# Moving a matrix-vector product from GpSimd to VectorE, one multiply-add at fixed places between weight conversions

## The chip, the cores and the metric

The kernel runs on one core of a Trainium2 chip. The metric is the device time of one execution in microseconds. The engines are TensorE (PE in the profile, its weight loads PEld), VectorE (DVE), ScalarE (ACT), GpSimd (POOL) and the sync engine (SP), which issues every DMA. Each runs its own instruction stream in order, and they meet only at semaphores.

## The reference

The input is one sequence of 256 tokens of width 1024, in float32. The first block has four layers of three sublayers each: FFN, mixer (MLA attention, differential attention, a Mamba-2 SSM, MLA again), FFN. Every sublayer is modulated by a vector that depends only on the conditioning input c:

```
cond = jax.nn.silu(c)                                  # (1, 1024)
mod = (cond @ w_mod[i] + b_mod[i]).reshape(-1, 3, 3, 1024)
shift, scale, gate = mod_j[:, 0, None, :], mod_j[:, 1, None, :], mod_j[:, 2, None, :]
y = fn(x * (1 + scale) + shift)
x = layernorm(DEEPNORM_ALPHA * x + weight * gate * y, g, b)
```

The matrix w_mod has 1024 x 9216 elements per layer, so each sublayer needs a matrix-vector product of 1024 x 3072. A second block follows (a hybrid of dilated attention and retention, cross-attention over a memory, an FFN) that has no modulation.

## The kernel before

Tokens lie along the free dimension and features on the 128 partitions. All weights are streamed. `Plan` cuts each matrix into blocks of 128 x 2048 float32 (1 MB): a column block is 256 columns of all eight row chunks, a block of an output projection is two row chunks of all 1024 columns. Every product is done in three float32r matmuls (high by high, high by low, low by high), so each block passes through this line:

- SP loads it into `raw[b % 4]` (`load`, line 524), once the block four before it has been converted by VectorE (`w_lo`).
- ScalarE rounds it into `whi[b % 2]` in two halves (`convert`, line 644), once TensorE is done with block b - 2.
- VectorE subtracts, `wlo = raw - whi`, in two halves (`convert`, line 971; the instruction is line 979).
- TensorE does 48 matmuls a block (line 1502 in `three`).

In a stage, turn i of VectorE and ScalarE converts block i + 2 of it. The FFN is a stage "in" of 22 column blocks and a stage "out" of 11 row blocks, written as loops of four blocks by `walk`, with what lies ahead and behind peeled. Mixers are unrolled: diff has 12 column blocks ahead of its attention and 4 row blocks behind it, the SSM 8 (z), 12 (xbc, where VectorE also does a convolution) and 1, the scan, and 8 row blocks, and MLA 3, a norm of the latents, 4 (q, each of six small DMAs), 2 (kv), the attention and 4 row blocks. `splits(g)` is VectorE's loop of conversions in a mixer, `projected` the one of an output projection, `attend` its part of an attention.

Between two sublayers stands a layer norm (`dve_ln`, `pe_ln`). VectorE computes the sum, the mean, the variance, then the modulated input (`hf`, `H_lo`), and last `residual()`, which signals `ax_ready`.

While sublayer s runs, the modulation product of s + 1 is accumulated in `mod_acc`, 128 x 2 x 1536, two halves. Row chunk k (128 rows) and half h are an item, numbered 2k + h, 16 in all. Each item is a DMA of 768 KB into `mod_w[:, h, :]` (`load_mod`, line 537). Load u waits until item u - 2, the last that used this half of the buffer, has been added: semaphore `mod_used`. GpSimd waits for the load, then does one small tick, one product by the element of `cond` of this row chunk (line 624, in place), and one add into `mod_acc` (line 627). It works whenever data is there. In `pe_ln`, TensorE sums over the partitions with 24 matmuls of one column (line 1570, `mod_sums`), which signal `mod_sum`; after that GpSimd begins on the next sublayer.

The order of SP's queue is written out. In an FFN, `load_mod` of the items 0 to 9 follows the weight loads at every second block of "in", items 10 and 11 stand ahead of the first "out" load, and the other four come among the "out" loads. In a mixer, each weight load ahead of the output projection is followed by one modulation load, and all that are left follow the second load of the output projection.

Of the kernel before, what the change touches and what calls it, by code (L numbers as in the profile page):

```python
# [26 lines left out]
ALU = mybir.AluOpType  # L27
AX = mybir.AxisListType.X
ds = bass.ds

P = 128
# [4 lines left out]
DEPTH = 4  # L36
# [279 lines left out]
def program(nc, plan, A, out, first, second):  # L316
# [4 lines left out]
    with ctx:  # L321
        def sem(name):
            return ctx.enter_context(nc.semaphore(name))
# [45 lines left out]
        pool_tick = at("pool_tick", [P, 16], room(64))  # L369
# [89 lines left out]
        mod_used = sem("mod_used")  # L459
        dve_step, act_step, pool_step = sem("dve_step"), sem("act_step"), sem("pool_step")  # L460
# [34 lines left out]
        def _(sp):  # L495
# [50 lines left out]
            for st in steps:  # L546
# [41 lines left out]
                if st.kind in ("mla", "diff", "ssm", "hyb", "xatt"):  # L588
                    nxt = st.args[0] + 1 if st.kind not in ("hyb", "xatt") else 10 ** 6
                    todo = [(nxt, k, half) for k in range(DC) for half in range(2)] if nxt < plan.mods else []  # L590
                    for g in st.lin.values():
                        for b in range(g.b, g.b + g.n):
                            load(b)

                            late = g is st.lin["out"] and b == g.b + 1
                            while todo and (late or b < st.lin["out"].b):
                                load_mod(*todo.pop(0))
                                if not late:
                                    break
# [6 lines left out]
        @block.gpsimd  # L606
        def _(pool):

            n = min(plan.mods, SUB * DEPTH)
            if n > 1:  # L610
                pool.wait_ge(s["cond_ready"], 1)
                with pool.Fori(1, n) as sub:
                    pool.wait_ge(s["mod_sum"], sub * 2)
                    for k in range(DC):
                        for half in range(2):
                            pool.wait_ge(mod_loaded[half], sub * 128 + 16 * (k + 1) - 128)

                            nc.gpsimd.tensor_tensor(pool_tick[:, 2 * k + half:2 * k + half + 1], cond[:, 0:1], cond[:, 0:1], ALU.add)  # L618
                            w = mod_w[:, half, :]
                            if k == 0:  # L620
                                nc.gpsimd.tensor_scalar(mod_acc[:, half, :], w, cond[:, 0:1], 1.0, ALU.mult, ALU.mult)\
                                    .then_inc(mod_used, 1)
                                continue
                            nc.gpsimd.tensor_scalar(w, w, cond[:, k:k + 1], 1.0, ALU.mult, ALU.mult).then_inc(pool_step, 1)  # L624
                            pool.wait_ge(pool_step, sub * 14 - 14 + 2 * (k - 1) + half + 1)
                            pool.wait_ge(mod_used, sub * 16 + 2 * k + half - 1)
                            nc.gpsimd.tensor_tensor(mod_acc[:, half, :], mod_acc[:, half, :], w, ALU.add)\  # L627
                                .then_inc(mod_used, 1)
# [331 lines left out]
        def _(dve):  # L960
# [19 lines left out]

            def coefficients(sub, n):
# [157 lines left out]
            def dve_ffn(st, n):  # L1139
# [17 lines left out]
                def turn(i, it=None):  # L1157
                    convert(g.b + i + 2, it)
                    if i % 2 == 1:
                        product(i // 2, it)  # L1160
                    if i % 2 == 0 and i >= 2:
                        product_lo(i // 2 - 1, it)

                walk(dve, g, turn)
                product_lo(FP - 1)
                projected(st)

            def projected(st):
                g = st.lin["out"]
                walk(dve, g, lambda i, it: None if it is None and i >= g.n - 2 else convert(g.b + i + 2, it), 1, 2)  # L1170


            def attend(n, heads, scale, kind):
# [62 lines left out]
                for i in range(heads + 4):  # L1236
                    if i < heads:
                        maxima(i)
                    if 1 <= i <= heads:
                        normal(i - 1)  # L1240
                    if i >= 4:
                        output(i - 4)

            def dve_mla(st, n):
                splits(st.lin["latent"])
# [16 lines left out]
                splits(st.lin["q"])  # L1262
                splits(st.lin["kv"])
# [10 lines left out]
                attend(n, MLA_H, 192.0 ** -0.5, "mla")  # L1274
                projected(st)

            def splits(g):
                for i in range(g.n):
                    convert(g.b + i + 2)

# [5 lines left out]
            def dve_diff(st, n):  # L1286
                splits(st.lin["qk"])
                splits(st.lin["v"])
                attend(n, 8, 64.0 ** -0.5, "diff")
# [11 lines left out]
            def dve_ssm(st, n):  # L1301
                splits(st.lin["z"])
# [79 lines left out]
                projected(st)  # L1382
# [581 lines left out]
```

## Time and profile before

| | |
|---|---|
| median of 3 runs | 3269.76 us (3255.11 to 3269.94) |
| span of the profiled execution | 3259.7 us |
| the profiled execution's own time | not on the page; the runs' median is 10.1 us over its span |
| TensorE busy | 2803.8 us (86%) |
| VectorE busy | 2262.1 us (69%) |
| ScalarE busy | 1272.2 us (39%) |
| GpSimd busy | 1080.1 us (33%) |
| DMA | 576.21 MB, mean 177 GB/s |

A row of the view by groups reads: line, engine, operation, output<-inputs, shapes, count, then busy us and mean ns of one, then the idle time ahead of them and what ended it. A row of the view by windows reads: start:end, length, then busy us (and instructions) of PE, PEld, DVE, ACT and POOL, then the granted TensorE clock (1.0 is full speed), the DMA engines' share and GB/s; a "sum" row adds several windows, their length first. A row of a timeline reads: start, us, engine, line, operation, and in brackets the idle time ahead of it and who ended it. In the view by waits it is: who waited for whom, us in total, times, longest.

### The profile page before, as it was taken

The numbers are of one execution on the slowest core, as the hardware profiler recorded it, in microseconds if no ns is written. First come the engines' busy times: TensorE is split into PE (matmuls) and PEld (weight loads), VectorE is DVE, ScalarE is ACT, GpSimd is POOL, SyncE is SP. The second block draws the span as 40 slices with busy tenths as digits, with TensorE's granted clock in tenths as the row PEclk, the third lists the DMA queues.
The fourth block names the chain that finished last, engine by engine and source line by source line (L and its number), as shares of the span: only waits on it lengthen the run. The fifth ranks groups of instructions, "written<-read, shape, count | busy, mean of one in ns | idle before, by whom it ended". The sixth has DMA issues, their size and how long they took to land.

```text
span 3259.7 us, 52310 instructions
## 1 busy us (share of the span) xinstructions
PE 2803.8 (86%) x20687; PEld 2661.0 (82%) x20687; DVE 2262.1 (69%) x2608; ACT 1272.2 (39%) x1667; POOL 1080.1 (33%) x510
## 2 busy tenths in 40 slices
PE   3996689989885998997889899999579988869797
PEld 3996489989884998997864899899559988569797
DVE  6677667777788777787766677775866555674554
ACT  2433344344334443443332443443234434344443
POOL 0564605627382263473800056263550000000000
PEclk7997789989897899997985899899678998779898
DMA  8774437657562575664720376475343544124352
GB/s 293 248 256 139 153 111 249 235 191 261 186 220 71 191 258 181 240 254 149 264 92 0 120 254 246 168 260 198 124 144 130 180 177 155 52 78 143 129 180 91
DMA packets 355092, 576.21 MB, mean 177 GB/s; under 512 B 20175, under 2 KB 295818, under 8 KB 354826
## 3 DMA queue, kind: packets, MB, share of 16 engines
q1 hardware_dynamic: 354954, 574.29, 50.6%
q8 instruction: 97, 1.59, 0.2%
q14 instruction: 41, 0.34, 0.0%
HBM read 573.20 MB, written 1.05 MB: 176 GB/s over the span
## 4 chain that ended last, share of the span: by engine, by line
PE 69%; DVE 21%; issue 6%; ACT 3%; SPq 1%; DMA 0%; DVEq 0%; ACTq 0%
PE ps L1502 62%; DVE wlo L979 4%; ACT whi L642 2%; PE ps L1815 1%; PE ps L1640 1%; DVE hf L1123 1%; DVE H_lo L1128 1%; DVE acc L1094 1%; PE ps L1806 1%; DVE acc L1010 1%; DVE z L1133 1%; DVE z L1110 1%; DVE ax L1022 1%; DVE conv L1317 1%; PE ps L1667 1%
## 5 line engine op out<-in xcount | busy, mean ns | idle before, releaser
L979 DVE TENSOR_TENSOR wlo<-raw,whi 128x1024 fp32r<-128x1024 f32 x804 | 1292.5, 1624 | 708.8 <-ACT whi L642 705.1
L1502 PE MATMUL ps<-H_hi,whi 128*128 128x256 f32 x4256 | 1236.4, 291 | 164.3 <-DVE H_lo L1128 75.7
L642 ACT ACTIVATE whi<-raw 128x1024 fp32r<-128x1024 f32 x804 | 846.1, 1058 | 1333.6 <-PE ps L1502 1327.2
L1502 PE MATMUL ps<-H_lo,whi 128*128 128x256 f32 x4256 | 1228.3, 289 | 0.0
L1502 PE MATMUL ps<-H_hi,wlo 128*128 128x256 f32 x4256 | 1227.4, 288 | 0.0
L1502 PEld LDWEIGHTS ps<-H_hi,whi 128*128 128x128 f32 x4256 | 842.1, 198 | 176.4 <-issue 137.8
L1502 PEld LDWEIGHTS ps<-H_lo,whi 128*128 128x128 f32 x4256 | 842.6, 198 | 0.0
L1502 PEld LDWEIGHTS ps<-H_hi,wlo 128*128 128x128 f32 x4256 | 841.3, 198 | 0.0
L627 POOL TENSOR_TENSOR mod_acc<-mod_acc,mod_w 128x1536 f32<-128x1536 f32 x154 | 619.1, 4020 | 25.2 <-POOL mod_w L624 25.2
L1502 PE MATMUL ps<-A_hi,whi 128*128 (+1 forms) x1880 | 538.4, 286 | 51.2 <-DVE A_lo L1256 28.1
L618 POOL TENSOR_TENSOR pool_tick<-cond 128x1 f32<-128x1 f32 x176 | 113.9, 647 | 1309.6 <-PE ps L1570 766.5
L1502 PE MATMUL ps<-A_hi,wlo 128*128 (+1 forms) x1880 | 535.6, 285 | 0.0
L1502 PE MATMUL ps<-A_lo,whi 128*128 (+1 forms) x1816 | 517.8, 285 | 0.0
L1502 PEld LDWEIGHTS ps<-A_hi,whi 128*128 128x128 f32 x1880 | 365.1, 194 | 55.5 <-DVE A_lo L1256 28.9
L1502 PEld LDWEIGHTS ps<-A_hi,wlo 128*128 128x128 f32 x1880 | 364.9, 194 | 0.0
L1502 PEld LDWEIGHTS ps<-A_lo,whi 128*128 128x128 f32 x1816 | 352.9, 194 | 0.1
L624 POOL TENSOR_SCALAR mod_w<-mod_w,cond 128x1536 f32<-128x1536 f32 x154 | 319.3, 2073 | 0.0
L1570 PEld LDWEIGHTS ps<-K,mod_acc 128*128 128x128 f32 x576 | 111.0, 290 | 23.0 <-DVE mod_acc L1048 20.2
L1570 PE MATMUL ps<-K,mod_acc 128*128 128x1 f32 x576 | 106.4, 315 | 19.9 <-DVE mod_acc L1048 19.9
L1640 PE MATMUL ps<-KN,QN 128*128 128x128 f32 (+3 forms) x192 | 55.1, 472 | 42.8 <-DVE QRp L1273 28.3
L1101 DVE SCALAR_TENSOR_TENSOR z<-ps,gw,ax 128x256 f32<-128x256 f32 x96 | 44.9, 478 | 65.4 <-PE ps L1502 65.4
L681 ACT ACTIVATE prob<-prob,stat 128x128 f32<-128x128 f32 x80 | 34.8, 445 | 135.0 <-DVE stat L1197 135.0
(278 smaller groups left out, 2304.7 us busy)
## 6 DMA issues: line engine op xcount, KB each, us to landing
raw<-in_ffn_w_in_dram SPq DMA_DIRECT2D x176, 1024.0 KB, 5.1
mod_w<-in_w_mod_dram SPq DMA_DIRECT2D x180, 768.0 KB, 6.2
raw<-in_ffn_w_out_dram SPq DMA_DIRECT2D x88, 1024.0 KB, 6.0
raw<-in_w_gate_up_dram SPq DMA_DIRECT2D x22, 1024.0 KB, 5.0
raw<-in_ssm_w_in_dram SPq DMA_DIRECT2D x20, 1024.0 KB, 7.0
raw<-in_w_in_dram SPq DMA_DIRECT2D x14, 1024.0 KB, 4.9
raw<-in_diff_w_in_dram SPq DMA_DIRECT2D x12, 1024.0 KB, 5.9
raw<-in_w_down_dram SPq DMA_DIRECT2D x11, 1024.0 KB, 4.9
```

Source lines behind the costliest of these rows:

```text
L618: nc.gpsimd.tensor_tensor(pool_tick[:, 2 * k + half:2 * k + half + 1], cond[:, 0:1], cond[:, 0:1], ALU.add)
L624: nc.gpsimd.tensor_scalar(w, w, cond[:, k:k + 1], 1.0, ALU.mult, ALU.mult).then_inc(pool_step, 1)
L627: nc.gpsimd.tensor_tensor(mod_acc[:, half, :], mod_acc[:, half, :], w, ALU.add)\
L642: return nc.scalar.activation(dst, src, ACT.Copy)
L681: i = nc.scalar.activation(prob[:, h % 4, m * width + a:m * width + b], src, ACT.Exp, bias=stat[:, h % 4, 4 + 2 * m + t:5 + 2 * m + t], sc ...
L979: tt(wlo[b % 2][:, r], raw[b % RAW][:, r], whi[b % 2][:, r].bitcast(F32), ALU.subtract).then_inc(w_lo, 1)
L1010: link(tt(f, f if q > 1 else sq[:, 0:2, :], sq[:, 2 * q:2 * q + 2, :], ALU.add))
L1022: i = ts(ax[:, c, :], z[:, c, :], G2[:, c:c + 1], B2[:, c:c + 1], ALU.mult, ALU.add)
L1101: stt(z[:, c, :], ybank(g, c), gw[:, c:c + 1], ax[:, c, :], ALU.mult, ALU.add).then_inc(s["z_ready"], 1)
L1502: m = pe.matmul(out, l, r, start=first and i == 0, stop=last and i == 2, skip_group_check=rest)
L1570: m = pe.matmul(ps[:, b, o:o + 1], mod_acc[:, c // 12, c % 12 * P:c % 12 * P + P], ones[:, 0:1], start=True, stop=True)
L1640: m = pe.matmul(ps[:, b, o:o + keys], q[:, t * P:t * P + P], k[:, 0:keys], start=i == 0, stop=i == len(terms) - 1)
```

## The change

GpSimd's loop is replaced by one clearing of the accumulator for each sublayer, which waits for `mod_sum` and for the residual's `ax_ready` and signals `mod_clear`. VectorE does each item in one instruction, `mod_acc = mod_w * cond + mod_acc` (`modulate`), at a fixed place: in the FFN's "in" stage ahead of the conversion in every even turn from 2, items 10 and 11 in turn 0 of "out", items 12 to 15 in later turns of "out"; in MLA and diff one item behind each conversion of `splits` and one in each turn of `attend` until none is left; in the SSM eight items in z and eight behind the turns of the output projection. The FFN's and the other mixers' order of loads stays as it is; in the SSM the modulation loads now stand behind the loads of z and of the output projection.

```diff
-                            late = g is st.lin["out"] and b == g.b + 1
-                            while todo and (late or b < st.lin["out"].b):
+                            late = st.kind != "ssm" and g is st.lin["out"] and b == g.b + 1
+                            early = g is st.lin["z"] or g is st.lin["out"] if st.kind == "ssm" else b < st.lin["out"].b
+                            while todo and (late or early):
                                 load_mod(*todo.pop(0))
                                 if not late:
                                     break
...
-                with pool.Fori(1, n) as sub:
+                for sub in range(1, n):
                     pool.wait_ge(s["mod_sum"], sub * 2)
-                    for k in range(DC):
-                        for half in range(2):
-                            pool.wait_ge(mod_loaded[half], sub * 128 + 16 * (k + 1) - 128)
...
+                    pool.wait_ge(s["ax_ready"], sub)
+                    nc.gpsimd.memset(mod_acc[:, :, :], 0.0).then_inc(mod_clear, 1)
...
+            def modulate(sub, k, half, it=None):
+
+                u = 16 * sub + 2 * k + half
+                loaded = 128 * (sub - 1) + 16 * (k + 1)
+                dve.wait_ge(mod_loaded[half], loaded if it is None else loaded + 16 * it)
+                if k == 0:
+                    dve.wait_ge(mod_clear, sub)
+                dve.wait_ge(mod_used, u - 1 if it is None else u - 1 + 2 * it)
+                c = cond[:, k:k + 1] if it is None else cond[:, ds(it + k, 1)]
+                stt(mod_acc[:, half, :], mod_w[:, half, :], c, mod_acc[:, half, :], ALU.mult, ALU.add).then_inc(mod_used, 1)
...
                 def turn(i, it=None):
+                    if mods and i >= 2 and i % 2 == 0:
+                        modulate(mods, (i - 1) // 4, (i - 1) // 2 % 2, it)
                     convert(g.b + i + 2, it)
...
+                def turn_out(i, it):
+                    if mods and i == 0:
+                        modulate(mods, 5, 0)
+                        modulate(mods, 5, 1)
+                    if mods and i in (1, 3):
+                        modulate(mods, 6, i // 2, it)
+                    if it is not None or i < g.n - 2:
+                        convert(g.b + i + 2, it)
...
-            def splits(g):
+            def splits(g, mods=()):
                 for i in range(g.n):
                     convert(g.b + i + 2)
+                    if mods:
+                        modulate(*mods.pop(0))
```

`attend` and the SSM's `projected` get the same last two lines at the end of each turn.

## Rows read from the trace of the kernel before

**Rows 1.** The page: busy shares, and the chain by engine.

```profile
PE 2803.8 (86%) x20687; PEld 2661.0 (82%) x20687; DVE 2262.1 (69%) x2608; ACT 1272.2 (39%) x1667; POOL 1080.1 (33%) x510
PE 69%; DVE 21%; issue 6%; ACT 3%; SPq 1%; DMA 0%; DVEq 0%; ACTq 0%
```

**Rows 2.** By windows: norm, "in" and "out" of FFN 11, GpSimd idle.

```profile
2467.20:2483.30 16.10, 10.91 (x51) 10.33 (x52) 14.44 (x31) 8.09 (x13) 0.00 (x0) 0.58 0.20 66
2483.30:2611.60 128.30, 128.30 (x1057) 128.30 (x1058) 75.71 (x87) 59.23 (x69) 0.00 (x0) 0.99 0.53 177
2611.60:2675.50 63.90, 63.77 (x530) 63.36 (x528) 28.29 (x31) 22.86 (x22) 0.00 (x0) 1.00 0.60 217
```

**Rows 3.** By windows: sum of the "in" stages of the other seven FFNs.

```profile
sum 913.10, PE 906.26 PEld 903.28 DVE 714.45 ACT 413.06 POOL 496.10; mean PE 129.47 PEld 129.04 DVE 102.06 ACT 59.01 POOL 70.87
```

**Rows 4.** By windows: sum of the seven "out" stages.

```profile
sum 464.00, PE 449.14 PEld 447.72 DVE 291.70 ACT 160.14 POOL 200.77; mean PE 64.16 PEld 63.96 DVE 41.67 ACT 22.88 POOL 28.68
```

**Rows 5.** By windows: sum of six norms ahead of an FFN.

```profile
sum 102.50, PE 59.90 PEld 56.97 DVE 93.97 ACT 45.77 POOL 10.27; mean PE 9.98 PEld 9.49 DVE 15.66 ACT 7.63 POOL 1.71
```

**Rows 6.** By windows: sum of the four norms ahead of a mixer.

```profile
sum 72.20, PE 41.13 PEld 39.16 DVE 67.30 ACT 32.70 POOL 15.17; mean PE 10.28 PEld 9.79 DVE 16.83 ACT 8.18 POOL 3.79
```

**Rows 7.** Timeline of GpSimd in the first FFN.

```profile
160.57 3.52 POOL L627 TENSOR_TENSOR mod_acc<-mod_acc,mod_w 128x1536 f32<-128x1536 f32 x1 [0.16 <-POOL mod_w L624]
```

**Rows 8.** Timeline of VectorE at the same place.

```profile
160.72 4.45 DVE L979 TENSOR_TENSOR wlo<-raw,whi 128x1024 fp32r<-128x1024 f32 x1 [1.65 <-ACT whi L642]
```

**Rows 9.** VectorE's instructions on the tile wlo: min/median/max ns, first and last start.

```profile
L979 DVE TENSOR_TENSOR wlo<-raw,whi x804: 1204/1226/4539, 44.9 to 3228.1; 128x1024 fp32r<-128x1024 f32 x161
```

**Rows 10.** By windows: MLA's start to scores, diff's, SSM's z, SSM's out, second MLA.

```profile
279.00:382.40 103.40, 56.08 (x340) 51.12 (x340) 77.72 (x59) 33.66 (x46) 68.25 (x34) 0.80 0.44 147
890.30:984.50 94.20, 77.94 (x592) 76.84 (x592) 77.56 (x48) 34.40 (x42) 79.04 (x35) 0.90 0.64 217
1515.30:1589.00 73.70, 63.97 (x463) 63.26 (x464) 62.21 (x43) 26.24 (x32) 60.07 (x27) 0.85 0.68 231
1797.70:1845.40 47.70, 47.70 (x389) 47.61 (x387) 25.80 (x34) 16.98 (x17) 0.00 (x0) 0.97 0.44 149
2294.20:2401.50 107.30, 58.83 (x341) 54.34 (x341) 81.33 (x59) 33.62 (x46) 69.02 (x36) 0.74 0.44 147
```

**Rows 11.** By waits: the sync engine's DMA queue.

```profile
SPq L535 <- DVE wlo L979: 2287.2, 342, 128.8
SPq L544 <- POOL mod_acc L627: 380.7, 63, 12.4
```

**Rows 12.** Timeline of the DMA queue at the first MLA's start.

```profile
275.38 0.34 SPq L544 DMA_DIRECT2D mod_w<-in_w_mod_dram  x1
275.76 3.00 SPq L535 DMA_DIRECT2D raw<-in_mla_w_q_up_dram  x6
```

**Rows 13.** By groups: VectorE's first multiply-adds, GpSimd's first product, ScalarE's conversion.

```profile
L1048 DVE SCALAR_TENSOR_TENSOR mod_acc<-mod_first,cond,mod_acc 128x1536 f32<-128x1536 f32 x12 | 21.4, 1814 | 1.2 <-DMA mod_first<-in_w_mod_dram 0.9
L621 POOL TENSOR_SCALAR mod_acc<-mod_w,cond 128x1536 f32<-128x1536 f32 x22 | 35.5, 1615 | 0.0
L642 ACT ACTIVATE whi<-raw 128x1024 fp32r<-128x1024 f32 x804 | 846.1, 1058 | 1333.6 <-PE ps L1502 1327.2 <-DMA raw<-in_ffn_w_in_dram 5.5 <-PE ps L1775 0.9
```

**Rows 14.** Timeline of VectorE in FFN 11: after the residual, and in turn 19.

```profile
2494.84 4.61 DVE L979 TENSOR_TENSOR wlo<-raw,whi 128x1024 fp32r<-128x1024 f32 x4
...
2602.50 0.68 DVE L1149 TENSOR_TENSOR am<-sg,ps 128x512 f32<-128x512 f32 x1
```

**Rows 15.** Tile raw, 1560 to 1593: five column blocks issued behind modulation loads.

```profile
DMA to landing us min/median/max: 6.7/7.4/8.1
```

**Rows 16.** Tile raw, 955 to 960: a row block behind a modulation load.

```profile
DMA to landing us min/median/max: 6.3/6.3/6.3
```

**Rows 17.** By windows: attention of the first MLA, of diff.

```profile
382.40:423.10 40.70, 36.55 (x120) 23.07 (x121) 22.89 (x63) 12.91 (x47) 15.25 (x9) 0.69 0.41 142
984.50:1046.20 61.70, 27.47 (x114) 17.77 (x112) 53.08 (x119) 25.36 (x84) 15.15 (x8) 0.67 0.25 90
```

More of the change, by code:

```diff
@@ L368, in program @@
         acc = at("acc", [P, 3, S], room(12 * S))
-        pool_tick = at("pool_tick", [P, 16], room(64))
         sq = at("sq", [P, DC, S], o_s1 + 4 * DC * S)
@@ L458, in program @@
         second_loaded = sem("second_loaded")
-        mod_used = sem("mod_used")
-        dve_step, act_step, pool_step = sem("dve_step"), sem("act_step"), sem("pool_step")
+        mod_used, mod_clear = sem("mod_used"), sem("mod_clear")
+        dve_step, act_step = sem("dve_step"), sem("act_step")
         stored = sem("stored")
@@ L610, in _ @@
             if n > 1:
-                pool.wait_ge(s["cond_ready"], 1)
-                with pool.Fori(1, n) as sub:
+                for sub in range(1, n):
                     pool.wait_ge(s["mod_sum"], sub * 2)
-                    for k in range(DC):
-                        for half in range(2):
-                            pool.wait_ge(mod_loaded[half], sub * 128 + 16 * (k + 1) - 128)
[L618 to L628, printed above, removed]
+                    pool.wait_ge(s["ax_ready"], sub)
+                    nc.gpsimd.memset(mod_acc[:, :, :], 0.0).then_inc(mod_clear, 1)
         @block.scalar
@@ L979, in convert, with next_mods @@
                     tt(wlo[b % 2][:, r], raw[b % RAW][:, r], whi[b % 2][:, r].bitcast(F32), ALU.subtract).then_inc(w_lo, 1)
+            def modulate(sub, k, half, it=None):
[7 more added lines that the diff above has]
+                stt(mod_acc[:, half, :], mod_w[:, half, :], c, mod_acc[:, half, :], ALU.mult, ALU.add).then_inc(mod_used, 1)
+            def next_mods(st):
+                nxt = st.args[0] + 1
+                return [(nxt, k, half) for k in range(DC) for half in range(2)] if nxt < min(SUB * DEPTH, plan.mods) else []
             def coefficients(sub, n):
@@ L1162, in turn, with projected, attend @@
                         product_lo(i // 2 - 1, it)
+                mods = st.args[0] + 1 if st.args[0] + 1 < min(SUB * DEPTH, plan.mods) else 0
                 walk(dve, g, turn)
                 product_lo(FP - 1)
-                projected(st)
-            def projected(st):
-                g = st.lin["out"]
-                walk(dve, g, lambda i, it: None if it is None and i >= g.n - 2 else convert(g.b + i + 2, it), 1, 2)
-            def attend(n, heads, scale, kind):
+                def turn_out(i, it):
[6 more added lines that the diff above has]
+                        convert(g.b + i + 2, it)
+                g = st.lin["out"]
+                walk(dve, g, turn_out, 1, 2)
+            def projected(st, mods=()):
+                g = st.lin["out"]
+                assert g.n <= 8
+                for i in range(g.n):
+                    if i < g.n - 2:
+                        convert(g.b + i + 2)
+                    if mods:
+                        modulate(*mods.pop(0))
+            def attend(n, heads, scale, kind, mods=()):
                 maps = 2 if kind == "diff" else 1
@@ L1242, in attend @@
                         output(i - 4)
+                    if mods:
+                        modulate(*mods.pop(0))
+                assert not mods
             def dve_mla(st, n):
-                splits(st.lin["latent"])
+                mods = next_mods(st)
+                splits(st.lin["latent"], mods)
                 idx = st.args[0] // 9
@@ L1261, in dve_mla @@
                 tt(KRp[:, :], rtmp[:, 0, 0, :], rtmp[:, 1, 0, :], ALU.add).then_inc(s["kr_ready"], 1)
-                splits(st.lin["q"])
-                splits(st.lin["kv"])
+                splits(st.lin["q"], mods)
+                splits(st.lin["kv"], mods)
                 cos2 = cosm[:, :].unsqueeze(1).to_broadcast([P, 2, S])
@@ L1273, in dve_mla @@
                     tt(QRp[:, 2 * i:2 * i + 2, :], rtmp[:, 0], rtmp[:, 1], ALU.add).then_inc(s["qr_ready"], 1)
-                attend(n, MLA_H, 192.0 ** -0.5, "mla")
+                attend(n, MLA_H, 192.0 ** -0.5, "mla", mods)
                 projected(st)
-            def splits(g):
+            def splits(g, mods=()):
                 for i in range(g.n):
                     convert(g.b + i + 2)
+                    if mods:
+                        modulate(*mods.pop(0))
             def fin_low(n, i):
@@ L1286, in dve_diff @@
             def dve_diff(st, n):
-                splits(st.lin["qk"])
-                splits(st.lin["v"])
-                attend(n, 8, 64.0 ** -0.5, "diff")
+                mods = next_mods(st)
+                splits(st.lin["qk"], mods)
+                splits(st.lin["v"], mods)
+                attend(n, 8, 64.0 ** -0.5, "diff", mods)
                 dve.wait_ge(s["mixed_out"], n["mixed_out"] + 8)
@@ L1301, in dve_ssm @@
             def dve_ssm(st, n):
-                splits(st.lin["z"])
+                mods = next_mods(st)
+                splits(st.lin["z"], mods)
                 g = st.lin["xbc"]
@@ L1381, in dve_ssm @@
                     tt(A_lo[:, r, :], Z[:, r, :], A_hi[:, r, :].bitcast(F32), ALU.subtract).then_inc(s["fin_lo"], 1)
-                projected(st)
+                projected(st, mods)
             def dve_hyb(st, n):
```

## The prediction

> **What bounds the kernel now.** I read the page's busy shares and chain first. TensorE is busy 86% of the span and carries 69% of the chain, VectorE 21% [rows 1]. So the kernel is a row of TensorE stages, joined by stretches where VectorE sets the time. The windows by stage show how far each stage is from its own floor. FFN number 11 has no modulation work beside it, and GpSimd is idle: its 22 "in" blocks take 128.3 us (5.83 a block), its 11 "out" blocks 63.9, the layer norm ahead of it 16.1 [rows 2]. The seven FFNs with GpSimd at work take 913.1 and 464.0 in sum [rows 3, 4], that is 15.0 and 16.7 more than seven clean ones. The six norms ahead of an FFN take 102.5, the four ahead of a mixer 72.2 [rows 5, 6]: 5.9 and 7.8 more than clean ones.
>
> The reason is in two timelines. GpSimd's add starts at 160.57 and takes 3.52; a VectorE conversion that starts at 160.72 takes 4.45 [rows 7, 8], while its median is 1.23 and its worst 4.54 [rows 9]. VectorE stands until GpSimd's instruction has ended. The mixers' first stages suffer most [rows 10]: GpSimd is busy 60 to 79 us in each window.
>
> The other view that matters is the sync queue's own: it waits 2287 us for conversions (that is prefetch held back by free buffers, harmless) and 381 us for GpSimd's add [rows 11]. The queue is in order. At a mixer's start a modulation load is issued at 275.38 and the q weights behind it at 275.76 [rows 12]: weight loads stand behind modulation loads, and these wait for `mod_used`.
>
> **What the change does to VectorE.** GpSimd's 154 adds, 154 products, 22 first products and 176 ticks go. Eleven times 16 = 176 multiply-adds come, at 1.81 us each [rows 13], 319 us in all. In FFN turns VectorE is busy 75.7 of 128.3 us [rows 2]; eleven of them add 20, and TensorE still hides them. So FFN "in" goes to the clean 128.3: -15.0. The norms go to the clean 16.1: -13.7. The clearing writes 3072 elements; no row shows a GpSimd memset of that size. The nearest is its product of 1536 in 1.6 us [rows 13]. Bounds 0 and 6, taken 3.1. It starts when the residual is done, 11.6 us after the stage's first matmul (2494.9 less 2483.3) [rows 2, 14]. In a mixer VectorE's item 0 waits for it, with block 3's conversion queued behind; ScalarE and TensorE have blocks 1 and 2 to work on meanwhile, so the wait itself costs only the start of the loop below.
>
> The Trainium skill, page "SBUF — State Buffer", section "Who interferes with whom", says that a VectorE instruction with two SBUF inputs contends with a GpSimd instruction that reads SBUF and not with one that only writes. By that rule the clearing delays no conversion. If it did lock like the adds do, it would meet block 2's conversion (2494.84 to 2496.05 for the first half [rows 14]); TensorE wants that half at about 2496.6, two blocks and 1.6 us of slow start after 2483.3. It would be 2.6 us late in each of 11 sublayers: +29.
>
> **What the change does to the sync queue.** This is the step that decides. In a mixer the queue issues block j, then modulation load j. Load j waits until item j-2 is used. Until now GpSimd used it when it landed. Now VectorE does it in turn j-2 of `splits`, right after it converts block j. So block j+1 is not issued before block j is converted: the lead of up to four blocks is gone, and each turn is a closed loop:
> - modulation issue, then weight issue: 0.38 (275.38 to 275.76), taken as 0.45 with the queue's waking [rows 12]
> - landing of a weight block behind a modulation load: 7.4 for column blocks, 6.7 to 8.1 [rows 15]; 6.3 for row blocks [rows 16]
> - ScalarE's first half 1.06 [rows 13], then two halves on VectorE, 2.3 (4.61 for four) [rows 14]: 3.4
> - the multiply-add: 1.8 [rows 13]
>
> Sum: 13.05 us a block for column blocks, 11.95 for row blocks, against 5.83 that TensorE needs. Counted from the stage's first matmul, item 0 is done at 16.6 (11.6 for the residual, 3.1 for the clearing, 1.8).
>
> Diff: blocks 3 to 11 are gated, so item 9 ends at 16.6 + 9 x 13.05 = 134. The two "out" blocks then land at 141 and 143.5, and their conversions with items 10 and 11 end at 150.4, where the first score is read; it stands at 94.2 now [rows 10]. +56.
>
> SSM, z: item 5 ends at 82, block 8 lands at 90, its TensorE block and the conversions of 9 and 10 (they land close behind) put the first convolution at 101.7, against 73.7 [rows 10]. +28. From there VectorE's convolution sets the pace in both kernels.
>
> SSM, out: the same loop. Blocks 3 to 7 are gated by items 8 to 12. Item 8 ends at 9.9, item 12 at 57.9, block 7 is converted at 68.2, item 15 (loaded after item 13 at 69.9) ends at 75.9, and only then does VectorE begin the norm's sums, 5.8 long: 81.7, against 48.5 (47.7 and 0.8) [rows 10]. +33.
>
> MLA: seven gated loads. Item 2 ends at 40.8, the norm of the latents ends at 48.5, then four loops of 12: item 6 at 93.2. The last landing (6.8), conversion and copies (3), the last kv block (6), copies and the last item (5.5) and the rotation (4) give 118.7; now 103.4 and 107.2 [rows 10]. +15.3 and +11.5, though VectorE's stretched norm and rotation get shorter.
>
> Attention: 7, 7 and 4 multiply-adds go between the heads, 33 us if nothing hides them. What goes is GpSimd's 15.2 us beside each [rows 17], 46 if all were on the path. Bounds +33 and -46; most of GpSimd's part falls in the first heads, where VectorE is needed. I take +4.
>
> FFN, from "in" to "out": modulation load (5,1) waits for (4,1), which VectorE does in turn 20, and the first "out" block stands behind it. In the clean FFN turn 20 begins at 2603.2, when the product at 2602.50 [rows 14] ends. The multiply-add ends at 2605.0, the block lands at 2611.8 (0.45 and 6.3), its first half is ready at 2614.1 and the gate that frees the bank at 2614.5; TensorE wanted it at 2611.6: 3.0 late. The second "out" block, converted next, holds the last product, which frees the other banks: 1.9. Out block 2 stands behind (6,0), which waits for (5,0), done after that product: 3.4. Sum 8.3, so an "out" of 72.2, against 66.3 [rows 4]. Seven times 128.3 + 72.2 is 1403.5, against 1377.1: +26.4, the -15.0 above in it. Bounds of the 8.3: 0, if the load is as quick as one that stands alone, and 11.
>
> **Sum.** FFN +26.4, norms -13.7, diff +56.2, SSM +28.0 and +33.2, MLA +26.8, attention +4: +161 on the span of 3259.7, so 3421. The page gives the profiled execution's span and no time of its own; the median of the runs, 3269.8, is 10.1 above it, and I keep that: 3431. The loops' landing (6.7 to 8.1) over some 31 gated loads is 22 us to each side.
>
> **Rivals.**
> - *Faster: the lead does not matter.* If loads still run ahead, only the lock goes. FFNs -31.7, norms -13.7, diff's 12 blocks at 5.83 and 2 more: -22, SSM z -23, MLA -25 each; attention +4: about 3134. For it: the collisions are plain [rows 7 to 9]. Against: the order of the queue. It decides where a landing behind a modulation load is below some 0.2 us (5.83 less the other terms), which no row is near. 5%.
> - *Only the mixers lose their lead.* The FFN transition is hidden: 58 less, 3373. It needs landings of 3 us or less, or banks that are free earlier. 15%.
> - *No net effect.* The lead stays, and VectorE pays for its 64 multiply-adds in the mixers in full (116 us), which eats the relief of 140: about 3250. 5%.
> - *Worse.* The clearing locks as well (+29), or TensorE, half idle in the loops, is granted the lower clock there (mean 0.58 in the norm [rows 2]) and ends each starved stage some 4 us later: about 3465. 10%.
> - The forecast: 65%.
>
> The range that holds 8 in 10 runs from 3355 to 3475. A measurement tells 0.5% (16 us) from no change. Faster by more 0.05, within 0.03, slower 0.92.
>
> **What would show it.** In the changed trace the diff's q, k and v weights are issued about 13 us apart, each right behind a modulation load, whose wait is for VectorE's multiply-add; ScalarE's conversions there wait for DMA instead of for TensorE. TensorE's blocks in that stage start 13 us apart. FFN "in" windows are 128.3, "out" windows about 72 with three gaps in the first three blocks. Norms are 16.1, conversions never above 1.3 us. I am wrong if the weights in the mixers are issued as far ahead as now.

## The result and the profile after

The changed kernel takes 3442.8 us (median of 4 runs, 3438.4 to 3444.4) against 3267.3 for the kernel before in the same sessions: ratio 1.054, with an interval of 1.052 to 1.056. It is slower by 175 us; the forecast was 3431, and 3355 to 3475 as its range. The span of the profiled execution is 3441.8 us, 182 more than before.

The relief that the change should bring is there, and the loss as well. First the page of the changed kernel: busy shares, the granted clock by slice, and two groups of instructions.

```profile
PE 2863.8 (83%) x20687; PEld 2715.7 (79%) x20687; DVE 2093.7 (61%) x2784; ACT 1264.8 (37%) x1667; POOL 29.5 (1%) x15
PEclk8997689999876899998795789999867998879898
L965 DVE TENSOR_TENSOR wlo<-raw,whi 128x1024 fp32r<-128x1024 f32 x804 | 972.0, 1223 | 1067.1 <-ACT whi L628 1066.6
L976 DVE SCALAR_TENSOR_TENSOR mod_acc<-mod_w,cond,mod_acc 128x1536 f32<-128x1536 f32 x176 | 318.3, 1812 | 5.1 <-DMA mod_w<-in_w_mod_dram 2.7
```

The shares of the chain on this page add up to under 30%, so windows and waits are read in its place. GpSimd went from 1080 us to 29.5; what is left of it is this group of the list by lines:

```profile
L614 POOL MEMSET mod_acc<- 128x3072 f32 x11 | 29.3, 2667 | 2442.6 <-DVE ax L1024 2442.6
```

VectorE's 804 conversions take 972 us in all (1.223 in the mean, none above 1.227) where they took 1292.5, because none is held up by GpSimd any more; the 176 multiply-adds give 318 of those 320 us back. VectorE's other instructions got shorter too, so it is 168 us less busy than before (2093.7 for 2262.1). TensorE has the same 20687 matmuls, and yet the time is 5% longer. What stalls is seen in the waits. Waits of the sync engine's queue, to be laid beside [rows 11] (total us, times, longest):

```profile
SPq L534 <- DVE wlo L965: 1679.4, 283, 86.5
SPq L543 <- DVE mod_acc L976: 1280.1, 149, 153.2
```

Waits of ScalarE, same columns. The wait for TensorE is harmless (its output buffers are in use); the others are new and stand for weights that came late:

```profile
ACT whi L628 <- PE ps L1531: 1103.2, 608, 10.5
...
ACT whi L628 <- DMA raw<-in_ffn_w_out_dram: 124.5, 20, 11.1
ACT whi L628 <- DMA raw<-in_diff_w_in_dram: 95.9, 9, 15.2
```

Where the 182 us are, by windows of the changed kernel. The columns are those of [rows 2]. The sums of the seven "in" and the seven "out" stages (an "out" from the last matmul of "in" to its own last), and one "out" alone:

```profile
sum 901.57, PE 901.55 PEld 900.13 DVE 610.77 ACT 383.89 POOL 18.67; mean PE 128.79 PEld 128.59 DVE 87.25 ACT 54.84 POOL 2.67
...
838.18:912.37 74.19, 66.36 (x532) 65.96 (x531) 42.22 (x41) 26.49 (x27) 0.00 (x0) 0.95 0.65 243
...
sum 521.91, PE 467.22 PEld 464.45 DVE 295.48 ACT 185.39 POOL 0.00; mean PE 66.75 PEld 66.35 DVE 42.21 ACT 26.48 POOL 0.00
```

The six norms ahead of an FFN, with the one after the SSM, and the four ahead of a mixer:

```profile
1999.33:2019.41 20.08, 11.41 (x54) 10.82 (x53) 18.20 (x41) 8.71 (x14) 0.00 (x0) 0.60 0.78 256
...
sum 99.36, PE 57.11 PEld 54.21 DVE 90.72 ACT 47.78 POOL 0.00; mean PE 9.52 PEld 9.03 DVE 15.12 ACT 7.96 POOL 0.00
...
sum 64.92, PE 42.17 PEld 39.95 DVE 58.02 ACT 32.36 POOL 0.00; mean PE 10.54 PEld 9.99 DVE 14.51 ACT 8.09 POOL 0.00
```

The windows of [rows 10]: diff's start to its first score, the SSM's z, its "out", and both MLAs:

```profile
928.71:1075.92 147.21, 94.93 (x592) 92.05 (x592) 60.27 (x61) 33.06 (x41) 2.67 (x1) 0.77 0.41 138
1614.70:1714.69 99.99, 68.99 (x453) 67.67 (x454) 46.35 (x50) 25.36 (x31) 2.66 (x1) 0.80 0.49 160
1920.94:1999.33 78.39, 58.45 (x386) 57.00 (x384) 34.17 (x29) 14.39 (x15) 0.00 (x0) 0.82 0.38 139
283.18:405.26 122.08, 60.67 (x340) 55.14 (x340) 60.11 (x68) 33.32 (x45) 2.67 (x1) 0.72 0.34 112
2458.02:2579.79 121.77, 61.19 (x341) 55.81 (x341) 60.11 (x68) 33.32 (x45) 2.67 (x1) 0.71 0.34 112
```

| part | before | after | difference | forecast |
|---|---|---|---|---|
| FFN "in", seven | 913.1 | 901.6 | -11.5 | -15.0 |
| FFN "out", seven | 464.0 | 521.9 | +57.9 | +41.4 |
| norms, ten | 174.7 | 164.3 | -10.4 | -13.7 |
| diff to first score | 94.2 | 147.2 | +53.0 | +56.2 |
| SSM z | 73.7 | 100.0 | +26.3 | +28.0 |
| SSM out | 47.7 | 78.4 | +30.7 | +33.2, with its norm |
| MLA starts | 210.7 | 243.9 | +33.2 | +26.8 |
| attention, three | 144.8 | 148.0 | +3.2 | +4 |
| sum | | | +182 | +161 |

The last stages, which carry no modulation, are as before. The times of the table are of one profiled execution of each kernel.

The closed loop is seen in the timeline of the diff's start. The sync queue (start us, duration, instruction):

```profile
959.40 0.34 SPq L543 DMA_DIRECT2D mod_w<-in_w_mod_dram  x1
959.78 0.43 SPq L534 DMA_DIRECT2D raw<-in_diff_w_in_dram  x1
971.75 0.34 SPq L543 DMA_DIRECT2D mod_w<-in_w_mod_dram  x1
```

VectorE in the same stretch:

```profile
967.64 2.36 DVE L965 TENSOR_TENSOR wlo<-raw,whi 128x1024 fp32r<-128x1024 f32 x2 [8.27 <-ACT whi L628]
969.91 1.81 DVE L976 SCALAR_TENSOR_TENSOR mod_acc<-mod_w,cond,mod_acc 128x1536 f32<-128x1536 f32 x1
```

Read it as a circle: the weight is issued at 959.78; ScalarE can begin at 966.55, VectorE converts at 967.64, adds until 971.72, and 0.03 us later the queue issues the next modulation load, with the next weight behind it. The turn is 12.35 us, for a block that TensorE finishes in 5.8.

### The profile page after: what moved, and what is told of

It is laid out like the page before. It is cut to its first block and busy times, and to the rows that moved or that the text cites. A ratio compares the mean times of both kernels' runs of the same rounds, so it can differ in the third digit from the quotient of the medians.

```text
span 3441.8 us, 51916 instructions
## 1 busy us (share of the span) xinstructions
PE 2863.8 (83%) x20687; PEld 2715.7 (79%) x20687; DVE 2093.7 (61%) x2784; ACT 1264.8 (37%) x1667; POOL 29.5 (1%) x15
## 5 line engine op out<-in xcount | busy, mean ns | idle before, releaser
L965 DVE TENSOR_TENSOR wlo<-raw,whi 128x1024 fp32r<-128x1024 f32 x804 | 972.0, 1223 | 1067.1 <-ACT whi L628 1066.6
L1531 PEld LDWEIGHTS ps<-H_hi,whi 128*128 128x128 f32 x4256 | 842.6, 198 | 151.3 <-issue 79.8
L1531 PE MATMUL ps<-A_hi,whi 128*128 (+1 forms) x1880 | 557.8, 297 | 132.2 <-DVE wlo L965 80.9
L1531 PE MATMUL ps<-A_hi,wlo 128*128 (+1 forms) x1880 | 550.6, 293 | 0.0
L1531 PE MATMUL ps<-A_lo,whi 128*128 (+1 forms) x1816 | 533.4, 294 | 0.0
L1531 PEld LDWEIGHTS ps<-A_hi,whi 128*128 128x128 f32 x1880 | 381.3, 203 | 141.3 <-issue 67.8
L1531 PEld LDWEIGHTS ps<-A_hi,wlo 128*128 128x128 f32 x1880 | 380.2, 202 | 0.0
L1531 PEld LDWEIGHTS ps<-A_lo,whi 128*128 128x128 f32 x1816 | 368.9, 203 | 0.1
L976 DVE SCALAR_TENSOR_TENSOR mod_acc<-mod_w,cond,mod_acc 128x1536 f32<-128x1536 f32 x176 | 318.3, 1812 | 5.1 <-DMA mod_w<-in_w_mod_dram 2.7
L1669 PE MATMUL ps<-KN,QN 128*128 128x128 f32 (+3 forms) x192 | 57.9, 506 | 32.6 <-DVE QRp L1298 15.3
L1625 PE MATMUL ps<-acc,K 128*128 128x256 f32 x36 | 20.4, 667 | 62.2 <-DVE acc L1013 62.2
L1157 DVE TENSOR_TENSOR A_lo<-am,A_hi 128x512 f32 (+1 forms) x99 | 68.3, 690 | 6.3 <-ACT A_hi L628 6.3
```

Of the source, the lines that this page charges most:

```text
L965: tt(wlo[b % 2][:, r], raw[b % RAW][:, r], whi[b % 2][:, r].bitcast(F32), ALU.subtract).then_inc(w_lo, 1)
L976: stt(mod_acc[:, half, :], mod_w[:, half, :], c, mod_acc[:, half, :], ALU.mult, ALU.add).then_inc(mod_used, 1)
L1157: tt(A_lo[:, r, :], am[:, j % 2], A_hi[:, r, :].bitcast(F32), ALU.subtract).then_inc(s["a_lo"], 1)
L1531: m = pe.matmul(out, l, r, start=first and i == 0, stop=last and i == 2, skip_group_check=rest)
L1625: pe.matmul(ps[:, 5, 0:S], ones, acc[:, 1, :], start=True, stop=True).then_inc(s[signal], 1)
L1669: m = pe.matmul(ps[:, b, o:o + keys], q[:, t * P:t * P + P], k[:, 0:keys], start=i == 0, stop=i == len(terms) - 1)
```

## The experiments

All were built on the changed kernel, except E5. Times are medians; ratios are to the kernel before, run on the same chip (E1 to E4 on one, where it took 3268.2 us, E5 to E7 on another, where it took 3265.0).

| run | us | ratio (interval) |
|---|---|---|
| E1 lead in mixers | 3197.5 | 0.979 (0.976 to 0.982) |
| E2 lead in FFN "out" | 3367.7 | 1.032 (1.029 to 1.035) |
| E3 both leads | 3123.6 | 0.956 (0.953 to 0.959) |
| E4 short multiply-add | 3345.8 | 1.025 (1.022 to 1.028) |
| E5 before, short GpSimd work | 3102.4 | 0.951 (0.949 to 0.952) |
| E6 E3 without clearing | 3119.5 | 0.955 (0.954 to 0.957) |
| E7 E4 with a small load | 3262.0 | 1.000 (0.998 to 1.001) |

**E1: the mixers' weights go ahead of the modulation loads.** My theory was that order in the sync queue, not VectorE's arithmetic, costs the mixers their time. Every modulation load of MLA and diff, and of the SSM's z, moves three weight blocks later. In the SSM's output projection two of the eight loads go ahead, in among the weights of xbc, and the other six go behind its last two weights. The number of instructions, their waits and VectorE's order stay.

```diff
-                            late = st.kind != "ssm" and g is st.lin["out"] and b == g.b + 1
-                            early = g is st.lin["z"] or g is st.lin["out"] if st.kind == "ssm" else b < st.lin["out"].b
-                            while todo and (late or early):
+                            j, o = b - st.lin[next(iter(st.lin))].b, b - og.b
+                            if st.kind == "ssm":
+                                n = 1 if 3 <= j < 13 or o == 6 else 5 if o == 7 else 0
+                            else:
+                                n = 16 if o == 1 else 1 if j >= 3 and o < 0 else 0
+                            for _ in range(min(n, len(todo))):
```

> The changed kernel, with one thing altered: in the mixers each modulation load stands three weight blocks later in the sync queue (in the SSM's output projection behind its last two loads), so that no weight block waits for a multiply-add of VectorE that comes after the conversion of the block ahead of it. VectorE's program is the same. Theory (lost lead of the weight loads): diff's start falls from 147 us to about 75, the SSM's z from 100 to about 53, its output projection from 78 to 48 and its norm from 20 to 16, both MLA starts from 122 to about 77: some -240, so about 3200. Rival (VectorE's own work between the conversions is the cost): VectorE does exactly what it did, so the stages stay within 10% and the time stays above 3400.

Measured 3197.5, 245 less than the changed kernel. Windows of E1: the diff's start, z, and "out", the same three stretches as above.

```profile
880.77:956.62 75.85, 73.51 (x592) 72.91 (x592) 60.79 (x60) 34.34 (x41) 2.67 (x1) 0.96 0.71 243
1492.08:1548.79 56.71, 56.71 (x453) 56.71 (x454) 46.56 (x50) 26.13 (x31) 2.67 (x1) 0.95 0.78 267
1753.98:1801.69 47.71, 47.71 (x389) 47.62 (x387) 35.60 (x32) 14.98 (x15) 0.00 (x0) 0.97 0.51 171
```

VectorE's busy time is the one of the changed kernel (60.8 against 60.3 us), TensorE's idle time is gone (2.3 of 75.9 against 52.3 of 147.2), and the DMA share is 0.71 in place of 0.41. The same work, issued in another order. Not all came out as written: z is 56.7 where 53 was expected and the MLA starts are 80.8 and 79.8 where 77 was, and the whole is 5 us better than -240. The sync queue of E1 now issues a weight per TensorE block:

```profile
916.42 0.34 SPq L543 DMA_DIRECT2D mod_w<-in_w_mod_dram  x1
916.80 0.60 SPq L534 DMA_DIRECT2D raw<-in_diff_w_in_dram  x1
922.18 0.34 SPq L543 DMA_DIRECT2D mod_w<-in_w_mod_dram  x1
```

The pairs look as before, a load and a weight behind it, but 5.76 us apart, and this weight is needed three blocks later.

**E2: the same for the FFN's "out".**

```diff
-                    def turn_out(i, it):
-                        load(g.b + i, it)
-                        if mods and i in (1, 3):
-                            load_mod(nxt, 6, i // 2, it)
-                    for half in range(2 * mods):
-                        load_mod(nxt, 5, half)
-                    walk(sp, g, turn_out, 1, 2)
+                    behind = {1: (10,), 3: (11,), 5: (12, 13), 8: (14,), 10: (15,)}
+                    for i in range(g.n):
+                        load(g.b + i)
+                        for u in behind.get(i, ()) if mods else ():
+                            load_mod(nxt, u // 2, u % 2)
```

> The changed kernel, with only the order of the sync queue in the FFN's output stage altered: out blocks 0 and 1 ahead of item 10, 2 and 3 ahead of item 11, 4 and 5 ahead of items 12 and 13, then 14 behind block 8 and 15 behind block 10. Theory: the three gaps at the start of the out stages close, seven FFNs go from 203 us each to about 193: -70, so about 3372, and the mixers stay. Rival (the two multiply-adds in turn 0 hold the conversions by themselves): the third gap stays, about 4 us, and the gain is 40 or less.

Measured 3367.7, 75.1 less than the changed kernel. The sum of its seven "out" windows, and one of them:

```profile
815.51:879.42 63.91, 63.78 (x533) 63.58 (x531) 38.19 (x37) 22.88 (x22) 0.00 (x0) 1.00 0.65 229
...
sum 447.36, PE 446.45 PEld 445.04 DVE 267.12 ACT 160.15 POOL 0.00; mean PE 63.78 PEld 63.58 DVE 38.16 ACT 22.88 POOL 0.00
```

521.9 less 447.4 is 74.5: the whole saving lies in these stages. They are the clean "out" of [rows 2] to 0.01 us, at clock 1.00, with the multiply-adds still in them.

**E3: both leads together.**

> Both orders of the sync queue altered, VectorE's program as in the changed kernel. Theory: the two gains add up, -310, so about 3130, and this is below the kernel before (3267) by 4%, because the collisions of VectorE with GpSimd are gone as well. Rival (what is won by the removed collisions is eaten by the 176 multiply-adds on VectorE): 3267 or more.

Measured 3123.6, faster than both kernels: 4.4% below before (4.1 to 4.7), 9% below the changed one. The two savings add up: 245.3 and 75.1 are 320.4, measured 319.3. So the multiply-adds' places in VectorE's program were not the fault; the places of their loads were.

**E4: is part of the loss the multiply-add's own length?** It goes over 8 of 1536 columns, all else stays (this leaves out nearly all of the modulation's arithmetic).

```diff
-                stt(mod_acc[:, half, :], mod_w[:, half, :], c, mod_acc[:, half, :], ALU.mult, ALU.add).then_inc(mod_used, 1)
+                stt(mod_acc[:, half, 0:8], mod_w[:, half, 0:8], c, mod_acc[:, half, 0:8], ALU.mult, ALU.add).then_inc(mod_used, 1)
```

> The changed kernel with each multiply-add over 8 of its 1536 columns (the modulation is left incomplete), all waits and the order of loads as they are. Theory: a gated turn gets shorter by the multiply-add's 1.75 us only, some 31 turns -54, the FFN transitions -25, attention -10: about -90, so about 3350. The turn of the loop in diff goes from 12.4 to 10.6. Rival (VectorE's added busy time is the cost): all of the 175 us over the kernel before comes back, and 3270 or less is measured.

Measured 3345.8: 97 less than the changed kernel, and still 2.5% over before. VectorE in the diff's start of E4:

```profile
947.44 2.36 DVE L965 TENSOR_TENSOR wlo<-raw,whi 128x1024 fp32r<-128x1024 f32 x2 [8.56 <-ACT whi L628]
949.72 0.22 DVE L976 SCALAR_TENSOR_TENSOR mod_acc<-mod_w,cond,mod_acc 128x8 f32<-128x8 f32 x1
959.27 2.36 DVE L965 TENSOR_TENSOR wlo<-raw,whi 128x1024 fp32r<-128x1024 f32 x2 [9.33 <-ACT whi L628]
```

The turns are 11.0 to 11.8 us where 10.6 was expected: 1.6 us went, but the landing became longer, 7.7 in the median against 6.8 (why was not tried). The multiply-add is 1.8 us of a circle of 12. Without it the diff's start is 133.2 us: 14.0 less than in the changed kernel, where E1's order takes 71.4 away. Over the whole kernel 97 us come back, of 175 lost against before and of 319 that E3's order wins.

**E7: the bytes ahead of the weight.** E4, and the modulation's DMA brings 8 columns of each row too. Issues, waits and order stay; the modulation's arithmetic and its bytes are left out.

```diff
-                sp.dma_start(mod_w[:, half, :], w[ds(row, P), :]).then_inc(mod_loaded[half], 16)
+                sp.dma_start(mod_w[:, half, 0:8], w[ds(row, P), 0:8]).then_inc(mod_loaded[half], 16)
```

> The kernel with the 8-column multiply-add (3345.8), and now the modulation's DMA brings 8 columns of each row as well; issues, waits and order stay. The modulation's arithmetic and bytes are left out, its place in SP's queue is kept. Theory (what the mixers and the FFN's 'out' lose is a weight that is issued only when a multiply-add is done and then lands behind 768 KB): a weight lands in about 4.9 instead of 7.4 us behind the load, 2.5 us in some 31 turns and as much in the FFNs' 'out' gaps, in all about -100, to 3250. Rival (the late issue alone costs, not the bytes ahead of the weight): within 1% of 3346.

Measured 3262.0, 84 less than E4. Landing of the weights in the diff's start, in the changed kernel, in E4 and in E7:

```profile
DMA to landing us min/median/max: 6.5/6.8/8.5
```

```profile
DMA to landing us min/median/max: 6.9/7.7/8.5
```

```profile
DMA to landing us min/median/max: 5.1/5.2/6.6
```

The 768 KB ahead of a weight cost it 2.5 us. Even with neither arithmetic nor bytes the kernel only comes back to before's time: what is left of the loop (issue, 5.2 of landing, 3.4 of conversions) is still 9 to 10 us a turn against 5.8. The diff's start shows the steps: 147.2 us in the changed kernel, 133.2 without the arithmetic, 113.4 without the bytes as well, and 75.9 in E1, with both but in the other order. How much the order alone costs in the whole kernel, E5 says.

**E5: what the modulation had cost in the kernel before.** GpSimd's product and add go over 8 columns, with all their waits (the modulation's arithmetic is left out).

```diff
-                            w = mod_w[:, half, :]
+                            w = mod_w[:, half, 0:8]
...
-                            nc.gpsimd.tensor_tensor(mod_acc[:, half, :], mod_acc[:, half, :], w, ALU.add)\
+                            nc.gpsimd.tensor_tensor(mod_acc[:, half, 0:8], mod_acc[:, half, 0:8], w, ALU.add)\
```

> The kernel before, in which GpSimd's product and its addition go over 8 columns instead of 1536; every instruction, wait and place in the queues stays. So this one leaves out nearly all of the modulation's arithmetic. Theory (the product and addition cost VectorE's conversions their time while both run, and nothing else of them is on the path): conversions of 4.5 us go to 1.22 us, and the time falls by what the stages lose where VectorE binds: FFNs about -32 (7 times 4.5), norms -11, mixers' starts the rest, to some 3130 to 3200. Rival (in the kernel before the modulation was nearly free, all of it behind other work): the time stays within 1% of 3268.

Measured 3102.4, 163 less than before. The direction was right; the size was above the range that I had written, in which the attention was left out (its three windows are 122.3 us here and 144.8 before). E5 and E7 both do almost no arithmetic, and E5 even moves all the bytes; the 160 us between them are the price of the closed loops when nothing stands in them but a small load. With the full load in them (E4) it is 243. Diff's start and its attention in E5, and one "out":

```profile
840.61:915.42 74.81, 73.08 (x589) 72.89 (x591) 40.56 (x49) 34.27 (x41) 16.26 (x42) 0.96 0.94 339
...
915.42:966.86 51.44, 27.29 (x119) 17.82 (x116) 43.20 (x118) 25.46 (x85) 0.00 (x0) 0.73 0.07 21
```

```profile
193.07:256.98 63.91, 63.78 (x533) 63.58 (x531) 28.30 (x31) 22.87 (x22) 3.18 (x6) 1.00 0.58 206
```

These us were lost through VectorE, and not only in conversions. It is busy 1800.6 us in E5 and was 2262.1 before. At the diff's start in the kernel before, two instructions on `z` beside a GpSimd add took 6.95 us; the same two in E5:

```profile
905.26 6.95 DVE L1133 TENSOR_TENSOR z<-z,std 128x1024 f32<-128x1024 f32 x2
```

```profile
846.89 2.36 DVE L1133 TENSOR_TENSOR z<-z,std 128x1024 f32<-128x1024 f32 x2
```

A rival would be the sync queue, since the modulation loads waited for GpSimd before too. In that window of the kernel before (890 to 985 us) ScalarE's conversions wait for TensorE alone (56.9 us) and never for DMA, so no weight came late there.

The same two stretches of the diff in E3:

```profile
848.38:923.58 75.20, 72.86 (x592) 72.25 (x592) 60.90 (x60) 34.35 (x41) 2.66 (x1) 0.97 0.70 245
...
923.58:982.32 58.74, 29.50 (x112) 19.56 (x113) 50.12 (x123) 25.35 (x84) 0.00 (x0) 0.65 0.32 112
```

E3 with all the arithmetic is 21 us above E5 with none. Its starts are as short (75.2 and 74.8); the attention is not: four multiply-adds stand between the diff's heads, 7.2 us of VectorE, and the window is 7.3 longer. In each MLA's attention it is 5.6 longer (41.0 and 40.9 against 35.4) for seven of them, 12.7 us. Together 18.5 of the 21 us. The multiply-add is thus nearly free under TensorE's stages, and in the attention, where VectorE binds, it costs 44% (MLA) to all (diff) of its length.

**E6: does the clearing hold VectorE up?** E3 without it: the first step of each chunk writes a plain product on VectorE.

```diff
-                    nc.gpsimd.memset(mod_acc[:, :, :], 0.0).then_inc(mod_clear, 1)
...
-                    dve.wait_ge(mod_clear, sub)
+                if k == 0 and it is None:
+                    ts(mod_acc[:, half, :], mod_w[:, half, :], c, None, ALU.mult).then_inc(mod_used, 1)
+                    return
```

> The version with both leads (3123.6), without GpSimd's clearing of the accumulator: the first step of each chunk writes a plain product on VectorE, and GpSimd does nothing. Theory (a clearing that only writes does not hold up VectorE): the same within 0.5%, 3108 to 3139, conversions stay at 1.22 us. Rival (the clearing locks VectorE out for its 2.7 us in each of 11 chunks): faster by about 29, to 3095.

Measured 3119.5, 0.13% below E3 (ratios of 0.955 and 0.956, with intervals that overlap). The rival's 29 us are not there; the clearing is hidden. (E6 even saves VectorE something, since 22 of the 176 items are now products of 1.02 us and not multiply-adds of 1.81.) In the list by lines the conversions of E6 have the mean that E3's have, 1.224 us:

```profile
L958 DVE TENSOR_TENSOR wlo<-raw,whi 128x1024 fp32r<-128x1024 f32 x804 | 974.9, 1224 | 752.7 <-ACT whi L621 751.0
```

The changed kernel shows it directly. At the diff's start the clearing runs beside two halves of a conversion, and both together take what two take elsewhere:

```profile
940.44 2.67 POOL L614 MEMSET mod_acc<- 128x3072 f32 x1 [216.16 <-DVE ax L1024]
```

```profile
940.24 2.35 DVE L965 TENSOR_TENSOR wlo<-raw,whi 128x1024 fp32r<-128x1024 f32 x2
```

The Trainium skill, page "SBUF — State Buffer", section "Who interferes with whom", says that a VectorE instruction with two SBUF inputs contends with a GpSimd instruction that reads SBUF and not with one that only writes it. The runs agree with both halves: the clearing, which only writes, stretched no conversion, and GpSimd's product and add, which read, stretched them up to 4.54 us before (1.27 at most in E5).

## Why the prediction was right

**The step that decides held.** Most of the diff's weights are issued 12.4 us apart (959.78 and 972.14), each right behind a modulation load, where 13.05 was forecast. The term that was off is the landing: 6.8 in the median, not the 7.4 of [rows 15]. Those five had been issued closer together; in the closed loop the queue holds one load and one weight and nothing else (that this is why was not tried). The first turn was longer (its weight took 8.8 to land) and so was the last, so that the nine average 12.8: item 0 ends 16.3 us after the stage's first matmul (forecast 16.6), item 9 at 131.2 (134), and the first score comes at 147.2 for 150.4. SSM z confirms it (100.0 for 101.7), with most turns of 12.3 for 13.05. So does "out", with turns of 11.9 for 11.95: with its norm it takes 78.4 and 20.1 now, 47.7 and 17.0 before, +33.8 where +33.2, and -0.9 for the norm, was forecast. Undoing the order alone in E1 gave all of it back.

**MLA, +33.2 for +26.8.** In the first MLA item 2 ends 39.7 us after the start (forecast 40.8), item 6 at 95.4 (93.2), and what follows takes 26.7, not 25.5. The chain of steps was the one forecast, and the turns behind the latents' norm were 11.4 to 12.0 (12 forecast). The 93.2 is a slip of the sum: 48.5 and four loops of 12 are 96.5. With 96.5 the forecast of an MLA start would have been 122.0, and 122.1 and 121.8 were measured. In part two errors cancel there: that norm in fact ended at 50.6, and the first of the four items came sooner behind it than a whole loop.

**Norms.** Nine of ten are 15.8 to 16.3, as forecast. The tenth, behind the SSM, is 20.1, since VectorE gets to the sums only when its last items are done; that is part of the forecast's "out", 81.7.

**FFN "in".** No gap is left (TensorE is busy 901.55 of 901.57 us). It averages 128.8 and not 128.3, with a granted clock of 0.98 in four of the seven. (Ten multiply-adds stand in it, not the eleven of the prediction; hidden as they are, this changed nothing.)

**FFN "out", the mis-sized term.** Forecast 72.2 a stage, measured 74.6: 16.5 us in seven, most of the miss of 21. The stalls in all were near the forecast: TensorE stands for 7.8 us a stage (521.9 less 467.2, by 7), against "8.3" in the sum. What had no term is TensorE's speed afterwards: it is busy 66.75 for the same matmuls that take 63.8 in E2, 3.0 us more. The window by parts, of the third FFN in the changed kernel:

```profile
838.18:850.00 11.82, 7.94 (x65) 7.74 (x65) 10.01 (x9) 5.54 (x7) 0.00 (x0) 1.00 0.22 72
850.00:862.00 12.00, 8.05 (x52) 7.85 (x52) 5.35 (x5) 4.01 (x4) 0.00 (x0) 0.76 0.99 402
862.00:874.00 12.00, 12.00 (x98) 12.00 (x97) 7.17 (x6) 4.24 (x4) 0.00 (x0) 0.95 0.97 375
874.00:912.37 38.37, 38.37 (x323) 38.37 (x321) 19.69 (x23) 12.71 (x12) 0.00 (x0) 1.00 0.58 205
```

TensorE idles 3.9 us in the first part at clock 1.00 and 4.0 in the second, and there the granted clock is 0.76, a mean of its two levels of 2.4 and 1.2 GHz. It stays below 1 for some of the third, where TensorE has work all the time (98 matmuls in 12 us; the last part has 101 in as long). A closer cut finds the stretch at the lower level:

```profile
857.00:863.00 6.00, 4.97 (x23) 4.98 (x24) 6.00 (x5) 2.57 (x3) 0.00 (x0) 0.50 1.02 415
```

The clock fell while TensorE stood (1.00 from 854 to 856, 0.58 from 856 to 858). When it went on at 858.03, its next 24 matmuls started 0.21 us apart and not 0.12, until 863.1: 2.3 us lost, of the 2.6 that this stage is busier than E2's. In the second FFN it happened twice, behind a stall of 2.5 us (14 matmuls) and behind one of 5.3 (23), and the stage was busy 67.6. The rival "worse" had priced this for the mixers alone. E2 shows the link: without the stalls the clock is 1.00 in all seven, and the 3.0 us go with the 7.8. Why the stall of 2.5 us brought the clock down in the second FFN and not in the third was not tried.

The stalls stand where they were put. The sync queue and ScalarE at the transition of the second FFN:

```profile
611.82 0.34 SPq L543 DMA_DIRECT2D mod_w<-in_w_mod_dram  x1
612.20 1.23 SPq L534 DMA_DIRECT2D raw<-in_ffn_w_out_dram  x2
```

```profile
618.62 2.00 ACT L628 ACTIVATE whi<-raw 128x1024 fp32r<-128x1024 f32 x2 [10.41 <-DMA raw<-in_ffn_w_out_dram]
```

ScalarE begins on the weight 6.4 us after its issue (6.3 forecast), having idled for 10.4. TensorE begins "out" 2.5 us after the end of its last "in" matmul, where in E2 the two overlap by 0.16: 2.7 late (3.0 forecast). Two more gaps follow, 1.3 and 4.0 in the third FFN (1.9 and 3.4 forecast). In part the forecast's sum was lucky: the gap of 1.3 stands in only four of the seven stages, and the last gap is 3.6 to 5.3, 4.5 in the mean.

**The offset.** I had added 10 us for what lies between span and median. In the changed kernel it is 1.0, and each profiled execution whose time is known took only 1.8 to 2.9 us more than its span: most of the 10 us was that a quick execution of the kernel before had been profiled. The span forecast was 3421, 21 short, and 9 of them were hidden by that. This part of the closeness of 3431 to 3443 is luck.

**Rivals.** "The lead does not matter" forecast 3134 on its own condition; E3, which restores the lead, measured 3124. The condition was false and its sum nearly right. "Only the mixers lose" fell, since "out" lost 58. "No net effect" needed the lead, and fell with it; even with the lead (E3) all the arithmetic costs 21 us, not 116. Of "worse", the clearing that locks fell in E6.

## What to carry to other kernels

When a consumer moves to another engine, look at who issues its loads: a prefetch behind a load that waits for the consumer lives in that consumer's loop. Here the four weight buffers ran empty because one smaller load stood ahead in an in-order queue. Put loads that wait for a late consumer some blocks behind the weights (three here, with four buffers), and read the result in the distance between weight issues, not in the queue's summed waits: these are 1280 us for the multiply-add in the slow kernel and still 446 in E3, where they cost nothing. And a stall of TensorE costs more than its length where the granted clock falls with it, here 3.0 us on 7.8.

## What the runs showed of the hardware

- GpSimd's product and add of 128x1536 cost the kernel before 163 us (E5), and VectorE was busy 461 us longer with them; its write-only clearing of 128x3072, 2.67 us long, costs nothing that E6 could measure.
- At the diff's start a weight of 1 MB that is issued right behind 768 KB on the same queue lands in 6.8 us (changed kernel, median) or 7.7 (E4), behind a load of 8 columns in 5.2 (E7). With three blocks of lead in E1 the diff's twelve weights land hardly faster (median 6.3, for 6.8 in the changed kernel), but nobody waits.
- Most of such a landing is bandwidth. At the third FFN's transition (829 to 842 us, 40 slices) the DMA engines stand idle until a modulation load and two weights are issued, 2.88 MB in all. Then they are busy to the full, at 170 to 340 GB/s in the first 1.6 us and mostly 400 to 450 from there, until all three have landed:

```profile
DMA  0000000000997789989999999999999994000000
GB/s 0 0 0 0 0 0 0 0 0 0 170 189 170 284 340 454 435 359 410 416 454 403 403 403 429 416 466 403 416 416 429 441 403 164 0 0 0 0 0 0
```

- VectorE's multiply-add takes 1.81 us for 1536 elements a partition and 0.22 for 8.
- After a stall of 4.0 us, 24 matmuls went at half the clock (0.21 us apart for 0.12), though two stalls of 2.5 and 1.3 us just before had left it at 1.00 (third FFN).
